# Hybrid attention and pooling block: one transpose for all meta keys, and V's high and low part in one stationary operand

## What is computed

```python
z = rms_norm(h, norm_gain[layer])
q, k, v, g_attn, u_pool, g_pool = split(z @ w_in)          # 16 query heads, 2 kv heads of 64
q, k = partial_rotary(q), partial_rotary(k)
# chunks of 64 tokens: each sees the 16 meta keys, the chunk before and itself (144 keys)
m = max(max(s), sink); p = exp(s - m)
p = p / (sum(p) + exp(sink - m)); o_attn = p @ v_window
o_pool = (trailing_mean(u_pool, 2/4/8/16) - u_pool) @ w_pool * pool_scale
gated = concat(silu(g_attn) * o_attn, silu(g_pool) * o_pool)
h = h + gated @ w_out;  return rms_norm(h, final_norm_gain)[:, N_META:]
```

## Time and profile before

| | us |
|---|---|
| median of the runs (3) | 1319.69 |
| lowest, highest | 1319.02, 1320.92 |
| the profiled execution | 1318.68 |
| its span, from the first to the last instruction | 1317.0 |
| TensorE busy (share of the span) | 1304.1 (99%) |
| VectorE busy | 731.6 (56%) |
| ScalarE busy | 529.0 (40%) |
| GpSimd busy | 109.0 (8%) |

### The profile page before, as it was taken

One profiled execution on the slowest core, in us unless ns is written; L12 is line 12 of the kernel. 1 busy time (PEld: TensorE's weight loads), 2 busy tenths in 40 slices (PEclk: granted clock), 3 DMA queues, 4 the chain that ended last, 5 costly groups with the idle time before them and its releaser, 6 DMA issues.

```text
span 1317.0 us, 17759 instructions
## 1 busy us (share of the span) xinstructions
PE 1304.1 (99%) x6437; PEld 1078.3 (82%) x6437; DVE 731.6 (56%) x1029; ACT 529.0 (40%) x1202; POOL 109.0 (8%) x130
## 2 busy tenths in 40 slices
PE   9999999999999999999999999999999999999997
PEld 9788888888888888888887888888888888888886
DVE  6644443576767674346456535356766767533634
ACT  7532222344444443225345222225444445322423
POOL 2122121100000001000001212120000000000000
PEclk9999999999999999999999999999999999999999
DMA  9511101000000005434532211110011011333452
GB/s 349 186 53 40 62 33 64 32 33 32 33 32 33 32 33 178 157 127 160 175 128 94 67 48 48 48 48 33 33 33 48 32 33 33 99 127 110 160 168 103
DMA packets 30416, 109.90 MB, mean 83 GB/s; under 512 B 3424, under 2 KB 3456, under 8 KB 30368
## 3 DMA queue, kind: packets, MB, share of 16 engines
q1 hardware_dynamic: 22032, 79.18, 17.4%
q0 software_dynamic: 8336, 30.05, 6.6%
HBM read 96.63 MB, written 12.58 MB: 83 GB/s over the span
## 4 chain that ended last, share of the span: by engine, by line
PE 97%; DMA 1%; DVE 1%; ACT 0%; issue 0%; POOL 0%; POOLq 0%
PE ps L1029 19%; PE ps L1030 19%; PE ps L1031 19%; PE ps L1270 9%; PE ps L1271 9%; PE ps L1269 9%; PE ps L1183 3%; PE ps L1216 2%; PE ps L1240 1%; PE ps L1239 1%; PE ps L1241 1%; PE ps L1224 1%; DMA xr<-in_x 1%; PE ps L1066 1%; PE ps L1040 1%; PE ps L1090 1%
## 5 line engine op out<-in xcount | busy, mean ns | idle before, releaser
L1029 PE MATMUL ps<-zh,wsplit 128*128 128x512 f32 x1072 | 423.2, 395 | 0.1
L1030 PE MATMUL ps<-zl,wsplit 128*128 128x512 f32 x1072 | 418.8, 391 | 0.0
L1031 PE MATMUL ps<-zh,wsplit 128*128 128x512 f32 x1072 | 417.7, 390 | 0.0
L711 DVE TENSOR_TENSOR wsplit<-wraw,wsplit 128x1024 fp32r<-128x1024 f32 x132 | 196.5, 1489 | 233.4 <-ACT wsplit L454 233.4
L1029 PEld LDWEIGHTS ps<-zh,wsplit 128*128 128x128 f32 x1072 | 201.2, 188 | 46.7 <-DVE wsplit L711 0.6
L1031 PEld LDWEIGHTS ps<-zh,wsplit 128*128 128x128 f32 x1072 | 201.4, 188 | 43.3
L1030 PEld LDWEIGHTS ps<-zl,wsplit 128*128 128x128 f32 x1072 | 201.4, 188 | 40.7
L454 ACT ACTIVATE wsplit<-wraw 128x1024 fp32r<-128x1024 f32 x132 | 141.0, 1068 | 225.2 <-PE ps L1271 218.7
L1270 PE MATMUL ps<-wsplit,gsh 128*128 128x512 f32 x512 | 202.7, 396 | 0.0
L1269 PE MATMUL ps<-wsplit,gsh 128*128 128x512 f32 x512 | 199.3, 389 | 0.3 <-DVE gsl L959 0.3
L1271 PE MATMUL ps<-wsplit,gsl 128*128 128x512 f32 x496 | 196.9, 397 | 0.0
(11 more groups left out here) (152 smaller groups left out, 1322.3 us busy)
## 6 DMA issues: line engine op xcount, KB each, us to landing
wraw<-in_wo SPq DMA_DIRECT2D x64, 512.0 KB, 3.2
wraw<-in_wa SPq DMA_DIRECT2D x36, 512.0 KB, 3.2
wraw<-wc SPq DMA_DIRECT2D x16, 512.0 KB, 3.3
wraw<-in_wb SPq DMA_DIRECT2D x16, 512.0 KB, 3.2
rows<-in_x POOLq DMA_DIRECT2D x16, 512.0 KB, 4.2
xr<-in_x POOLq DMA_DIRECT2D x12, 512.0 KB, 5.5
curaw<-in_wu SPq DMA_DIRECT2D x8, 512.0 KB, 7.7
wc<-cout POOLq DMA_DIRECT2D x8, 512.0 KB, 7.4
```

The source lines that it names most:

```text
L711: ve.tensor_tensor(wl[:, slot, 0:size], wraw[:, slot, 0:size], wh[:, slot, 0:size].bitcast(F32), ALU.subtract).then_inc(w_lo, 1)
L1029: te.matmul(ps[:, PB[bank], :], w_h, rhs_z(zh, tb, k), start=k == 0, stop=False)
L1030: te.matmul(ps[:, PB[bank], :], w_h, rhs_z(zl, tb, k), start=False, stop=False)
L1031: last = te.matmul(ps[:, PB[bank], :], w_l, rhs_z(zh, tb, k), start=False, stop=k == KT - 1)
```

## The change

Meta keys: the normalised probabilities of the meta keys go into a tile of their own, pmeta (128 x 4 x 2 x 16), and one transpose turns all four query groups at once into 128 partitions. ScalarE's and VectorE's copies out of PSUM then take the groups one by one from partitions 32u to 32u + 31, and ScalarE makes the second copy from SBUF. Sums: V's high and low part lie side by side in one tile vhl, for each kv two blocks of 64 columns (kv 0: high, low; kv 1: low, high). Two matmuls per kv give, for each, the high part's product in one half of the partitions and the low part's in the other, in a bank per kv (XB = OB, SPARE), and the meta keys' product goes to a third bank (MB = 3). ScalarE copies the two low products into osum (low_sums, between the exponentials of kv 0 and kv 1), VectorE adds the meta bank and the two high products to it, and GpSimd multiplies osum by the gates and sets o_gate. The factor 0.5 that L942 had is taken into V. The scores are moved into three banks, with a semaphore s_side between the two scores that share bank 2, and the maxima take two reductions. On VectorE scan and pooled product move from the head of the next chunk to the end of their own, ahead of the additions. On TensorE the wait for o_gate moves from ahead of the transposes to behind the first 24 matmuls of the projection. The diff, cut to its core:

```diff
+        XB, MB = (OB, SPARE), 3
...
         def score_tile(u, kv):
-            return ps[:, 2 * kv + u // 2, u % 2 * KEYS:u % 2 * KEYS + KEYS]
+            return ps[:, kv, u * KEYS:u * KEYS + KEYS] if u < 3 else ps[:, 2, kv * KEYS:kv * KEYS + KEYS]
...
-                with pool.Fori(0, NCH // 2) as pair:
-                    for slot in range(2):
-                        n = NCH * h + 2 * pair + slot
-                        c = 2 * pair + slot
-                        settle(pool)
-                        pool.wait_ge(s_done, n + CREDIT)
-                        gp.tensor_copy(kw[:, META + CH * slot:META + CH * slot + CH], qk[:, c, 0, :]).then_inc(ks_in, 1)
+                def window_keys(c):
+                    pool.wait_ge(s_done, NCH * h + c + CREDIT)
+                    gp.tensor_copy(kw[:, META + CH * (c % 2):META + CH * (c % 2) + CH], qk[:, c, 0, :]).then_inc(ks_in, 1)
+                window_keys(0)
+                for c in range(NCH):
+                    if c + 1 < NCH:
+                        window_keys(c + 1)
+                    pool.wait_ge(o_sum, 2 * (NCH * h + c + 1))
+                    gslice = gates[:, 0:HT, c * CH:c * CH + CH]
+                    gp.tensor_tensor(gslice, osum[:, :].rearrange("p (j t) -> p j t", t=CH), gslice, ALU.mult).then_inc(o_gate, 1)
...
-                sc.activation(vtok[:, :, :].rearrange("p m f -> p (m f)"), ps[:, 0:2, :].rearrange("p b n -> p (b n)"), ACT.Copy).then_inc(v_tok, 1)
+                sc.activation(vtok[:, :, :].rearrange("p m f -> p (m f)"), ps[:, 0:2, :].rearrange("p b n -> p (b n)"), ACT.Copy, scale=0.5).then_inc(v_tok, 1)
...
-                def exponents(n):
+                def low_sums(n):
+                    act.wait_ge(o_done, n + 1 + CREDIT)
+                    act.wait_ge(o_gate, n + CREDIT)
+                    sc.activation(osum[0:HD, :], ps[HD:P, XB[0], :], ACT.Copy)
+                    sc.activation(osum[HD:P, :], ps[0:HD, XB[1], :], ACT.Copy).then_inc(o_low, 1)
+                def exponents(n, between=None):
                     act.wait_ge(s_negm, n + 1)
                     for kv in range(2):
@@ -616,6 +633,8 @@
                                 act.wait_ge(s_sarg, n + 1)
                                 sc.activation(esink, sarg, ACT.Exp)
                         i.then_inc(s_exp, 1)
+                        if kv == 0 and between is not None:
+                            low_sums(between)
...
-                        sc.activation(vh[lo_p:hi_p, 0:4:3, :], vtok[lo_p:hi_p, 2 * g + sub // 2, :].rearrange("p (k d) -> p k d", k=2),
+                        sc.activation(vhl[lo_p:hi_p, 0:4:3, :], vtok[lo_p:hi_p, 2 * g + sub // 2, :].rearrange("p (k d) -> p k d", k=2),
...
-                        sc.activation(ptm[0:32, :], ps[0:32, PTM, :], ACT.Copy).then_inc(pt_hi, 1)
-                        sc.activation(ptm[64:96, :], ps[0:32, PTM, :], ACT.Copy).then_inc(pt_hi, 1)
+                        for u in range(4):
+                            i = sc.activation(ptm[0:32, u * P:u * P + P], ps[32 * u:32 * u + 32, PTM, 0:P], ACT.Copy)
+                        i.then_inc(pt_hi, 1)
+                        act.wait_ge(pt_hi, 4 * n + 3)
+                        sc.activation(ptm[64:96, :], ptm[0:32, :].bitcast(F32), ACT.Copy).then_inc(pt_hi, 1)
                         copy_out(1)
                         if not (last and sub == 3):
-                            exponents(n + 1)
+                            exponents(n + 1, between=n)
                             split_hi(h, A_TILES + GROUP_BLOCKS * g + sub + 2, sub % 2)
                 with act.Fori(0, NG - 1) as g:
                     attend_group(g, False)
                 attend_group(NG - 1, True)
+                low_sums(NCH * (h + 1) - 1)
...
-                    scores = ps[:, 0:4, 0:2 * KEYS].rearrange("p b (w s) -> p b w s", w=2)
-                    ve.tensor_reduce(mx, scores, AXX, ALU.max).then_inc(s_max, 1)
-                    dve.wait_ge(s_max, n + 1)
+                            cols = slice(CH + META * kv, 2 * CH + META * kv)
+                            for empty in (ps[:, kv, 0:3 * KEYS].rearrange("p (w s) -> p w s", s=KEYS)[:, :, cols], score_tile(3, kv)[:, cols]):
+                                ve.tensor_scalar(empty, empty, cst[:, 6:7], None, ALU.add).then_inc(s_mask, 1)
+                        dve.wait_ge(s_mask, 4)
+                    by_head = mx.rearrange("p (k u) -> p k u", u=4)
+                    ve.tensor_reduce(by_head[:, :, 0:3], ps[:, 0:2, 0:3 * KEYS].rearrange("p k (u s) -> p k u s", s=KEYS), AXX, ALU.max).then_inc(s_max, 1)
+                    ve.tensor_reduce(by_head[:, :, 3], ps[:, 2, 0:2 * KEYS].rearrange("p (k s) -> p k s", s=KEYS), AXX, ALU.max).then_inc(s_max, 1)
+                    dve.wait_ge(s_max, 2 * n + 2)
...
+                            pr, at_meta = probs[:, :, half * KPITCH:half * KPITCH + 2 * CH], META0 + META * half
+                            ve.tensor_tensor(pmeta[:, :, half, :], probs[:, :, at_meta:at_meta + META],
+                                             rden[:, heads].unsqueeze(2).to_broadcast([P, 4, META]), ALU.mult)
+                            ve.tensor_tensor(pr, pr, rden[:, heads].unsqueeze(2).to_broadcast([P, 4, 2 * CH]), ALU.mult).then_inc(p_ready, 1)
...
+                        ve.tensor_tensor(vhl[lo_p:hi_p, 1:3, :], vtok[lo_p:hi_p, 2 * g + sub // 2, :].rearrange("p (k d) -> p k d", k=2),
+                                         vhl[lo_p:hi_p, 0:4:3, :].bitcast(F32), ALU.subtract).then_inc(vw_lo, 1)
...
+                        for kv in range(2):
+                            dve.wait_ge(pt_hi, 4 * n + kv + 1)
+                            ve.tensor_tensor(ptl[:, kv, :], ps[:, PTB[kv], :], pth[:, kv, :].bitcast(F32), ALU.subtract)
+                        dve.wait_ge(pt_hi, 4 * n + 4)
+                        for u in range(4):
+                            i = ve.tensor_tensor(ptm[32:64, u * P:u * P + P], ps[32 * u:32 * u + 32, PTM, 0:P],
+                                                 ptm[0:32, u * P:u * P + P].bitcast(F32), ALU.subtract)
+                        i.then_inc(pt_lo, 1)
+                        if not (last and sub == 3):
+                            maxima(n + 1)
+                        gate_tile(1)
+                        if sub >= 2:
+                            i = 2 * g + sub - 2
+                            for tb in range(NTB):
+                                dve.wait_ge(pb_free[tb], FREES * h + HT + i + 1 + CREDIT)
+                            ve.scalar_tensor_tensor(gates[:, HT + i, :], pooled[:, sub - 2, :], stat[:, bass.ds(56 + i, 1)],
+                                                    gates[:, HT + i, :], ALU.mult, ALU.mult).then_inc(p_gate, 1)
+                        else:
+                            ut = PT * h + 2 * g + sub
...
+                        dve.wait_ge(o_low, n + 1)
+                        ve.tensor_tensor(osum[:, :], ps[:, MB, :], osum[:, :], ALU.add).then_inc(o_meta, 1)
+                        dve.wait_ge(o_meta, n + 1)
...
+                            own = slice(HD * kv, HD * kv + HD)
+                            ve.tensor_tensor(osum[own, :], ps[own, XB[kv], :], osum[own, :], ALU.add).then_inc(o_sum, 1)
...
-                        dve.wait_ge(o_done, n + 1 + CREDIT)
-                        gslice = gates[:, 0:HT, bass.ds((4 * g + sub) * CH, CH)]
-                        ve.scalar_tensor_tensor(gslice, ps[:, OB, :].rearrange("p (j t) -> p j t", t=CH), 0.5, gslice, ALU.mult, ALU.mult).then_inc(o_gate, 1)
...
-                    for u in range(4):
-                        for kv in range(2):
+                    for a, b in ((0, 3), (1, 0), (2, 1), (3, 2)):
+                        for u, kv in ((a, 0), (b, 1)):
                             rows_kv = slice(kv * HD, kv * HD + HD)
                             window = slice(META * (1 - kv), META * (1 - kv) + KEYS)
+                            if (u, kv) == (3, 0):
+                                pe.wait_ge(s_side, n + 1)
                             last = te.matmul(score_tile(u, kv), qk[rows_kv, c, 1 + 2 * u:3 + 2 * u, :].rearrange("p j t -> p (j t)"),
                                              kw[rows_kv, window], start=True, stop=True)
+                            if (u, kv) == (3, 1):
+                                last.then_inc(s_side, 1)
                     last.then_inc(s_done, 1)
...
                         project(slot, 0, 0, KT)
+                        pe.wait_ge(o_gate, n + CREDIT)
                         if h == 0 and sub < 2:
...
                         pe.wait_ge(p_ready, 2 * n + 2)
-                        pe.wait_ge(o_gate, n + CREDIT)
                         transposes(1)
                         bank_free(0, ahead=1)
-                        for u in range(4):
-                            te.transpose(ps[0:32, PTM, u * P:u * P + P], probs[:, u, META0:KPITCH], ident[:, :])
```

(12 more changed lines are left out.)

53 lines of the change are left out of this document (23 added, 30 removed).

## The result

The changed kernel takes 1362.31 us (median of 4 runs, 1359.2 to 1365.39) where the kernel before takes 1319.57 us in the same series: a ratio of 1.032, with an interval from 1.030 to 1.035. It is slower, as forecast, but by 43 us instead of 17, and outside the range. The profiled execution is the slowest of the four: 1365.39 us, span 1363.7. It stands against 1318.68 us of the profiled execution before, so there are 46.7 us to account for.

The account below looks back on a forecast made before the run. TensorE, busy for 99% of the span, was taken to bound the kernel. 1318.7 - 25.1 (TensorE's saved work) + 31.1 (stalls at o_gate) + 12.6 (ends of halves) = 1337.3 us, given as 1337; range 1320 to 1356.

Parts of the forecast that it names:

- What bounds it: TensorE, busy for 99% of the span: each matmul taken away is worth its full spacing, 25.1 us in all.
- the 30 places named: TensorE's waits for o_gate behind the projection's first 24 matmuls: 16 stalls of 1.55 us, 14 of 0.45, 31.1 together.
- GpSimd's price: GpSimd's gate product over 128x512 takes 1.30 us, the additions taking nothing from it through the shared ports.
- Rival (a): GpSimd's gate product takes 1.86 us as its row stands, 19 us more in all: 1356 us; chance 15%.
- The ends of the halves: Ahead of the output projection, gsl_first is queued behind the sixteenth chunk's gate: a 6.3 us stall, twice, 12.6 us.
- I cost them at nothing: Small meta copies and subtractions on ScalarE and VectorE end 0.4 to 0.9 us later, within 1.7 us of slack: 0.
- T: End of a chunk's last sum on TensorE, from which the chain to o_gate is timed; 310.19 in the chunk followed.
- Two copies of 512 columns in a row take 1.09: ScalarE's two copies of the low sums, between the exponentials of the two kv, take 1.09 us.
- two in a row of 1.29: Two of VectorE's three additions ahead of GpSimd's gate take 1.29 us, of 2.01 us for all three.
- the short chain: Sums to o_gate in a group's third and fourth chunk, through copies, additions and GpSimd's gate: a stall of 0.45 us.
- The long chain: Sums to o_gate in a group's first and second chunk, scan and pooled product ahead of the additions: 1.55 us stall.
- Rival (b): The wait moves to p_ready, as VectorE's normalisation stands still during GpSimd's gate: 9 us more, 1346 us; chance 15%.

Follow-up runs that it names:

- the filled kernel: Changed kernel plus matmuls of no use where TensorE stands still ahead of o_gate and at each half's end, all waits kept; 1354.72 us, ratio 1.026.
- the kernel with the copies first: Changed kernel with ScalarE's copies of the low sums ahead of all exponentials instead of behind the first four; 1356.18 us, ratio 1.028.

## Why the prediction was right or wrong

**What bounds it and the direction: right.** TensorE's 99% was the reason why 25 us could be saved, and the meta part bears out that it is worth about its full spacing: 10.8 us between the medians for the 10.4 worked out, less 1.5 for its two gaps. The stalls stand in the 30 places named, with GpSimd's gate as their releaser, and the ends at the two places named.

**GpSimd's price and the port: right.** 1.27 us (mean of 32) for the 1.30, with VectorE held as long. Also gsl_first, which took 1.86 in the earlier trace rows, takes 1.27 with no VectorE instruction ahead of it. Rival (a) falls by this; that the time came out nearer to its 1356 than to 1337 has other reasons. The rule of the Trainium skill that was cited (SBUF — State Buffer, "SBUF: two separate sides") agrees down to an instruction of four columns, held 1.25 us.

**The ends of the halves: right**, 6.27 us of gap for 6.3, and the run with gsl_first early shows the queue as their cause.

**"I cost them at nothing": the first step that failed.** The four copies and the copy behind them take 1.76 us instead of the 1.2 of the two before, the four subtractions 1.19 instead of 0.68: the last subtraction ends 0.67 us ahead of the sums, 1.06 later than before. I had weighed 0.4 to 0.9 against the 1.7 us of slack that the sums leave, and that was nearly right for the sums. But the maxima stand behind the subtractions on VectorE, and for them I counted only their own 0.4 to 0.5 against 0.9 of slack. Both delays add up on the same queue: the maxima come 1.14 us later against the sums than in the earlier trace rows, 0.2 more than there was. The exponentials then start at T - 0.30 instead of T - 0.50, the copies at T + 1.38 instead of T + 1.04. The scan is behind the maxima too, at T + 0.20 and T - 0.16 instead of T - 0.44. The kernel without the meta part gives the price: 0.3 us in each of 30 stalls.

**"Two copies of 512 columns in a row take 1.09", "two in a row of 1.29": mis-sized terms.** Both were read from pairs on the same 128 partitions, whose ends and starts overlap by 0.1. The new pairs go from one half of the partitions to the other and don't overlap: 1.20 and 1.41 us. The trace before already had such a pair in the same chunk, two copies to different partitions, 0.60 apart:

```profile
305.23 0.57 ACT L657 ACTIVATE ptm<-ps 32x512 fp32r<-32x512 f32 x1
305.83 0.58 ACT L658 ACTIVATE ptm<-ps 32x512 fp32r<-32x512 f32 x1
```

The copies also start 0.12 behind the end of the fourth exponential, where the fifth, which stood there before, started 0.03 ahead of it. So the short chain is T + 6.1 instead of T + 5.6, and the stall with its refill 0.97 instead of 0.45. Worked out from the rows: 0.34 (the copies' start) + 0.11 + 0.13 - 0.08 (the hand-overs and GpSimd) = 0.50.

**The long chain: mis-sized by the scan.** Additions at T + 4.0 instead of T + 3.26 in the first chunk: 0.64 from the scan's start, 0.17 from the product that starts 0.27 behind it instead of 0.10, less 0.08 for a small copy that this half doesn't have. It makes 2.35 with refill for the 1.55. In the second chunk the scan starts 0.36 earlier against T and the product follows 0.24 sooner, which is why its stall is 0.6 less.

**The last chunks: left out.** I wrote that the 15 matmuls between scores and sums hide the small operands, and named the price if that cover were gone, up to 0.9 us. In the sixteenth chunk these 15 are still there (513.84 to 517.37), but no scores follow the transposes, and they take some 1.4 us elsewhere. The 0.67 us that the small operands have left in other chunks become a gap of 0.75 us, twice. The slack of 1.7 us was that of a chunk with scores. Every kernel with the meta part has it, the one without it doesn't.

**The clock: left out.** The earlier trace rows and the rest of the trace before have TensorE without gaps in the attention stage, so no row showed what the granted clock does behind one. I priced a stall as its own length and a refill only. The low clock costs 7.6 us by the medians of the filled kernel and some 11 in the profiled execution.

**Rival (b)** was priced as 9 us on top; it was not that, but it named rightly what is late next: with the wait moved back, p_ready is late by nearly as much as o_gate.

In sum: +13.8 in the stalls, +0.6 at the ends, +1.5 at the last sums and some 11 through the clock make 26.9 of the 28.1 us between forecast and profiled execution. 1.2 us stay without a place.

## What to carry to other kernels

Before an edit is costed at nothing, follow the queue of each engine that it touches to the end: a slack can be spent once, and two harmless delays on the same queue were a stall thirty times over. When an in-order engine gets work that another engine waits for, ask what stands ahead of it there and what stands behind; moving the wait or the work in the queue moved the stall but didn't remove it. A change of two parts should be run as two changes: here one part alone is 0.9% faster, the other 2.8% slower.

## What the runs showed of the hardware

- On ScalarE and VectorE an instruction that starts at another partition than the one before didn't overlap it in these traces: two 64x512 copies 0.61 us apart, two 64x512 additions 1.41 in all, where two on the same 128 partitions took 1.09 and 1.29. Small copies of 32x128 stand 0.28 apart, each some 0.27 long. It is the place and not the width: ScalarE's and VectorE's two instructions that split V alternate between partitions 0 to 63 and 64 to 127 behind instructions of 128, and in the change they overlap by 0.1 in all 32 cases at 0 and by nothing in all 32 at 64.
- In the attention stage the granted clock falls to 1.2 GHz behind gaps of TensorE of 2.2 us and more, but not behind each: in five of six gaps of 2.2 to 2.7 us of the change, in four of six in the kernel with the copies first, in one of six in that with the wait put back and in one of six in that with gsl_first early, though the gaps are as long there. Behind every gap of 3.6 us or more it fell, or had fallen within it. In the change no gap of under 2 us was followed by a fall, but with the scan back several short ones close together were. What decides in between stays open.
- Behind a wait TensorE's next spacing is 0.34 instead of 0.23 us with 512 columns (23 of the 30 waits) and 0.14 instead of 0.12 with 256: 2.7 us that no view of waits shows.
